# An encoder layer with a mixture of experts: late conditioning chunks put ahead in three queues, a first chunk in halves, and the last expert block added on chip

## The chip, the cores and the metric

The kernel runs on one core of a Trainium2 chip. The metric is the device time of one execution in microseconds; less is better.

## The reference, cut to what matters

1536 tokens (a sequence of 512 and one of 1024) of width 1024, all in float32. Each sequence has its own conditioning row c.

```
mod = silu(c) @ w_ada + b_ada                 # six rows of 1024: shift1, scale1, gate1, shift2, scale2, gate2
h   = x * (1 + scale1) + shift1
z   = h @ w_in                                # 1536 columns: u | v | p
a   = gelu(u) * (w_spatial @ layernorm(gelu(v)) + b_spatial)    # chunks of 128 positions, 4 heads
b   = (windowed mean(p) - p) @ w_pool * pool_scale              # windows 2, 4, 8, 16
x   = layernorm(alpha * x + gate1 * ([a | b] @ w_out))
h   = x * (1 + scale2) + shift2
# each token goes to 2 of 32 experts (top group, top 2 inside it), rows grouped by expert in blocks of 128
y_e = (silu(h @ gate_e) * (h @ up_e)) @ down_e                  # gate, up: 1024 -> 512, down: 512 -> 1024
y   = sum over the token's two experts of weight * y_e
out = layernorm(alpha * x + gate2 * y)
```

## The kernel before

The five engines each run a program written out by hand, and meet only at semaphores; each engine takes its instructions in the order in which they stand. SyncE issues nearly all loads, GpSimd the indirect ones. A float32 product is made of three: each operand is split into a high half (rounded on ScalarE, the functions named high_) and a low half (subtracted on VectorE, the functions named low_), and TensorE adds high*high, high*low and low*high.

**Start.** Tiles of 128 tokens are taken in pairs, pair 0 first. For pair 0 the work goes by k, the eight slices of 128 input features: for each k a chunk of w_ada (load_ada0, in two DMAs; high_ada0; low_ada0; ada0_mm) gives shift1 and scale1 of these features, mod_columns turns them into columns, mods(k) adds the bias and modulates the slice of x, k_high and k_low split it, and the products with row k of w_in (load_win, high_win, low_win, three slots) follow. In front of k = 0 stand on TensorE some filler products (warm), the transposes of x tiles 0 and 1, the transpose of the bias columns, ada0_mm(0) and mod_columns(0). ScalarE copies the four banks of transposed x out of PSUM in between. VectorE's order from k = 0 on is mods(0), low_win(0), k_low(0), low_ada0(1), low_win(1), low_ada0(2), then for each k mods(k), low_win(k + 1), k_low(k), low_ada0(k + 2).

**Pairs 1 to 5.** TensorE makes u, p and v of the pair, and at four points of it, called u1, u3, p1 and p3, a late chunk: 256 further columns of w_ada for the other four rows of mod. There are twelve, n = 0 to 11: n = 3 at u3 of pair 1, n = 5 at p3 of pair 1, n = 7 at u3 of pair 2, n = 9 at p3 of pair 2. A late chunk is loaded (load_ada(n), which waits for late chunk n - 3 to be used), rounded (high_for), subtracted (low_late) and multiplied (late_mm, 16 products of 256 columns). ScalarE, VectorE and SyncE have the three steps each at a fixed place among their other work: VectorE's low_late(1, "u3") stands behind pool_p(0), the windowed sums of pair 0; high_for(i, "p3") stands behind high_h(2i + 2) on ScalarE and low_late(i, "p3") behind low_h(2i + 2) on VectorE, the split of the next pair's first tile; load_ada(9) stands behind load_x(7). After late_mm of u3, TensorE runs spatial(i - 1) and w_pool_mm(i - 1), and the latter waits for pool_p(i - 1).

**Norm, routing, experts.** The first layer norm goes tile by tile, with routing between. The rows h2 go to HBM, and a table gives for each block of 128 rows which rows it takes and where its result goes. The loop over blocks: gather(i) on GpSimd, transposes, gate_up(i) on TensorE, silu and gate, the transposes of the activations, down(i). take_y(i) on ScalarE copies the block's result to y_sb, and scatter(i) on GpSimd writes its rows to y_rows in HBM, one row for each token and choice. In the loop, TensorE runs gate_up(i), the transposes of block i + 1, down(i - 1), the transposes of block i's activations.

**End.** After the last block's down products ScalarE copies the result out, GpSimd scatters it, and SyncE loads y0 and y1 (the rows of both choices) for each of the twelve tiles in four slots once all scatters have landed. The twelve x1 tiles (fin) and four broadcast rows are loaded earlier, on the last blocks' progress. Meanwhile TensorE runs 36 filler products and ScalarE makes 24 diagonal matrices of the token weights (diag, in place of scaling rows). For each tile TensorE adds diag0 @ y0 + diag1 @ y1 in two halves of 512 columns, four plain float32 products, and VectorE gates it, adds alpha * x1, and makes the second layer norm; ScalarE squares and stores.

## Time and profile before

| | us |
|---|---|
| median of 3 runs | 1309.48 (1307.46 to 1310.91) |
| the profiled execution, its own time | 1311.05 |
| its span | 1309.3 |
| TensorE busy in it | 1242.0 (95%) |
| VectorE busy | 949.5 (73%) |
| ScalarE busy | 643.5 (49%) |
| GpSimd busy | 201.8 (15%) |
| granted TensorE clock, mean | 0.973 of full |

Start times count from the span's start. A wait in brackets behind an instruction is the idle time of its engine just before it, with what ended it. The pair stage runs from about 83 to 315, the norm and routing to about 530, the expert loop to 1225, the end from there. Records of products overlap: a product's record is longer than the distance to the next.

### The profile page before, as it was taken

To read this page: it belongs to the slowest core of one execution; us is meant where nothing else is said; L and a number is where in the kernel's file an instruction comes from. 1 tells how busy PE (TensorE), PEld (TensorE's weight loads), DVE (VectorE), ACT (ScalarE), POOL (GpSimd) and SP (SyncE) were. 2 spreads that over 40 slices of the span, in tenths; PEclk is the share of its full clock that TensorE was granted. 3 is DMA by queue.
4 is the path that set the end of the run, shared out by engine and by line. 5 is a ranking of instruction groups with operands and counts; after the bars stand their busy time and mean duration, and the time that the engine had idled before them with its cause. 6 is when DMAs were issued, how large, how long until landed. Compare 5 with 4: busy or idle time off the path is not lost.

```text
span 1309.3 us, 23427 instructions
## 1 busy us (share of the span) xinstructions
PE 1242.0 (95%) x6534; PEld 1026.6 (78%) x6535; DVE 949.5 (73%) x1180; ACT 643.5 (49%) x667; POOL 201.8 (15%) x242
## 2 busy tenths in 40 slices
PE   7998989999999999899999999999999999999890
PEld 6887979998888874778888888888888888888640
DVE  4765655556999987874788656664899988887297
ACT  5552221123222223655677545744777887776421
POOL 0011101000010011121112111111121221121122
PEclk8998989999999998899999999999999999999896
DMA  9942231015423456965999757765999999998983
GB/s 312 273 129 82 81 97 53 19 57 179 146 113 115 175 219 260 362 242 218 353 390 406 284 219 295 273 256 215 366 390 402 397 406 395 393 402 294 353 306 128
DMA packets 121646, 329.09 MB, mean 251 GB/s; under 512 B 12040, under 2 KB 43904, under 8 KB 121604
## 3 DMA queue, kind: packets, MB, share of 16 engines
q1 hardware_dynamic: 107412, 288.08, 59.1%
q0 software_dynamic: 12320, 34.15, 7.3%
q10 hardware_dynamic: 1872, 6.29, 1.2%
q8 instruction: 27, 0.44, 0.1%
q14 instruction: 15, 0.12, 0.0%
HBM read 296.97 MB, written 39.42 MB: 257 GB/s over the span
## 4 chain that ended last, share of the span: by engine, by line
PE 66%; DVE 16%; issue 11%; DMA 3%; POOL 2%; ACT 2%; DVEq 0%; ACTq 0%; SPq 0%; POOLq 0%
PE bank L1603 17%; PE bank L1605 17%; PE bank L1604 17%; PE bank L1903 2%; PE bank L1616 2%; PE bank L1618 2%; PE bank L1617 2%; POOL rstd L729 1%; PE bank L1927 1%; DVE h L1340 1%; DVE fin L1562 1%; DVE fin L1577 1%; ACT w_mid L945 1%; DVE gated L1558 1%; DMA sh2b<-mod_rows 1%
## 5 line engine op out<-in xcount | busy, mean ns | idle before, releaser
L1476 DVE TENSOR_TENSOR gu_l<-gu_raw,gu_h (+1 forms) x128 | 287.3, 2285 | 44.0 <-ACT gu_h L971 41.9
L1603 PE MATMUL bank<-gu_h,xT_h 128*128 (+1 forms) x624 | 247.3, 396 | 2.8 <-issue 1.4
L971 ACT ACTIVATE gu_h<-gu_raw (+1 forms) x128 | 238.9, 1928 | 14.1 <-issue 12.8
L1605 PE MATMUL bank<-gu_h,xT_l 128*128 (+1 forms) x624 | 243.8, 391 | 0.0
L1604 PE MATMUL bank<-gu_l,xT_h 128*128 (+1 forms) x624 | 243.4, 390 | 0.0
L1480 DVE TENSOR_TENSOR dn_l<-dn_raw,dn_h (+1 forms) x64 | 143.6, 2285 | 5.9 <-ACT dn_h L975 5.9
L1603 PEld LDWEIGHTS bank<-gu_h,xT_h 128*128 128x128 f32 x624 | 117.6, 188 | 26.7 <-issue 3.1
L1605 PEld LDWEIGHTS bank<-gu_h,xT_l 128*128 128x128 f32 x624 | 117.5, 188 | 25.1
L1604 PEld LDWEIGHTS bank<-gu_l,xT_h 128*128 128x128 f32 x624 | 117.7, 189 | 23.3
L1603 PE MATMUL bank<-dn_h,aT_h 128*128 (+1 forms) x312 | 125.5, 402 | 2.5 <-DVE aT_l L1490 2.5
L1605 PE MATMUL bank<-dn_h,aT_l 128*128 (+1 forms) x312 | 122.3, 392 | 0.0
L1604 PE MATMUL bank<-dn_l,aT_h 128*128 (+1 forms) x312 | 122.2, 392 | 0.0
L975 ACT ACTIVATE dn_h<-dn_raw (+1 forms) x64 | 119.0, 1914 | 0.1
L1616 PE MATMUL bank<-hT_h,win_h 128*128 128x256 f32 x384 | 110.0, 286 | 6.0 <-DVE hT_l L1135 5.5
L981 ACT ACTIVATE act_s<-bank 128x512 f32<-128x512 f32 x39 | 23.3, 597 | 181.2 <-PE bank L1605 181.2
L1618 PE MATMUL bank<-hT_h,win_l 128*128 128x256 f32 x384 | 107.8, 281 | 0.0
L1617 PE MATMUL bank<-hT_l,win_h 128*128 128x256 f32 x384 | 107.7, 281 | 0.0
L758 POOL DMA_INDIRECT y_rows<-y_sb,s_idx x39 | 72.6, 1862 | 192.1 <-ACT y_sb L1001 192.1
L1486 DVE TENSOR_TENSOR act_a<-bank,act_s 128x512 f32<-128x512 f32 x39 | 26.9, 691 | 79.5 <-ACT act_s L981 79.5
L1616 PEld LDWEIGHTS bank<-hT_h,win_h 128*128 128x128 f32 x384 | 72.9, 190 | 8.3 <-DVE hT_l L1135 6.5
L1603 PE MATMUL bank<-wout_h,z_h 128*128 128x512 f32 x192 | 77.4, 403 | 0.0
L1605 PE MATMUL bank<-wout_h,z_l 128*128 128x512 f32 x192 | 75.9, 395 | 0.0
(278 smaller groups left out, 2156.5 us busy)
## 6 DMA issues: line engine op xcount, KB each, us to landing
gu_raw<-in_w_gate_up SPq DMA_DIRECT2D x128, 1024.0 KB, 7.8
dn_raw<-in_w_down SPq DMA_DIRECT2D x64, 1024.0 KB, 7.5
y<-y_rows SPq DMA_DIRECT2D x24, 512.0 KB, 5.5
ada_raw<-in_w_ada SPq DMA_DIRECT2D x20, 512.0 KB, 7.1
ada_raw<-in_w_ada SPq DMA_DIRECT2D x10, 1024.0 KB, 5.6
win_raw<-in_w_in SPq DMA_DIRECT2D x8, 768.0 KB, 8.8
h_rows<-h SPq DMA_DIRECT2D x12, 512.0 KB, 2.6
fin<-x_rows SPq DMA_DIRECT2D x12, 512.0 KB, 9.3
```

The lines of the kernel that those rows point to most:

```text
L758: nc.gpsimd.indirect_dma_start(out=y_d, out_offset=bass.IndirectOffsetOnAxis(ap=s_idx[:, 0:1], axis=0), in_=y_sb[:], in_offset=None, bound ...
L971: nc.scalar.activation(gu_slot(gu_h, e, c), gu_slot(gu_raw, e, c), ACT.Copy).then_inc(S["gu_split_h"], 1)
L975: nc.scalar.activation(dn_slot(dn_h, e, c), dn_slot(dn_raw, e, c), ACT.Copy).then_inc(S["dn_split_h"], 1)
L1476: nv.tensor_tensor(gu_slot(gu_l, e, c), gu_slot(gu_raw, e, c), gu_slot(gu_h, e, c).bitcast(F32), ALU.subtract).then_inc(S["gu_split_l"], 1)
L1480: nv.tensor_tensor(dn_slot(dn_l, e, c), dn_slot(dn_raw, e, c), dn_slot(dn_h, e, c).bitcast(F32), ALU.subtract).then_inc(S["dn_split_l"], 1)
L1486: nv.tensor_tensor(act_a[:], ps[1][:], act_s[:], ALU.mult).then_inc(S["act_ready"], 1)
L1603: mm(out, lh, rh, start=start, stop=False)
L1604: mm(out, lh, rl, start=False, stop=False)
L1605: return mm(out, ll, rh, start=False, stop=stop)
L1616: mm(out, win_h[:, k, c], hT_h[s][:, k, :], start=start, stop=False)
L1617: mm(out, win_h[:, k, c], hT_l[s][:, k, :], start=False, stop=False)
L1618: return mm(out, win_l[:, k, c], hT_h[s][:, k, :], start=False, stop=stop)
```

## The change

1. **Late chunks.** load_ada(9) goes ahead of load_x(7) on SyncE; high_for(i, "p3") ahead of high_h(2i + 2) on ScalarE (for the last pair there is no such chunk); low_late(1, "u3") ahead of pool_p(0), and low_late(i, "p3") ahead of low_h(2i + 2), on VectorE.
2. **First chunk by halves.** The two DMAs of chunk 0 get a semaphore each, and rounding and subtraction are done in two halves. TensorE runs ada0_mm(0) ahead of the x transposes. Slice 0 of x is modulated straight out of PSUM; ScalarE copies the banks without it, two before k_high(0) and two after it. Row 0 of w_in is split in two parts (u columns first), and k_low(0) stands ahead of the second part.
3. **Last block.** It isn't scattered. clear_last, on GpSimd between gather(3) and scatter(0), writes zeros to the rows of y_rows that it would have written; this counts as one scatter, so every scatter and take_y waits for one more, and SyncE's loads of y0 and y1 wait for the clear and for the scatters of all blocks but the last. VectorE makes a 0/1 matrix onehot (which token each row of the last block belongs to) from an index row that GpSimd makes, and finds each row's weight through row_sel, its transpose on TensorE between the two halves of the last down product, and one small product. ScalarE scales the result into last_h, VectorE makes last_l, and TensorE adds onehot @ last_h and onehot @ last_l to every tile, four more products of 512 columns. The 36 filler products go; the diagonal matrices are made before the last block's result is taken.

```diff
+    " x_loaded xT_made x0_ready x0_used ada_first ada_h_made ada_l_made ada_made mod_hl_made mod_cols mod_made"
...
                 c, n = 2 * D + (k - KD) * ADA_N + m * P, P
-            sp.dma_start(ada0_raw[slot][:, :, m * P:(m + 1) * P], w_ada[:, :, c:c + n]).then_inc(ada_loaded[slot], 16)
+            sp.dma_start(ada0_raw[slot][:, :, m * P:(m + 1) * P], w_ada[:, :, c:c + n]).then_inc(S["ada_first"] if k + m == 0 else ada_loaded[slot], 16)
...
     load_ada(8)
+    load_ada(9)
     load_x(7)
-    load_ada(9)
     load_ada(10)
...
+    def clear_last():
+
+        pool.wait_ge(S["tab_ready"], 3)
+        st.done(pool.memset(y_sb[:], 0.0))
+        st.done(nc.gpsimd.tensor_copy(s_idx[:], table_s[:, bass.ds(column(last_block), 1)]))
+        st.sync()
+        nc.gpsimd.indirect_dma_start(out=y_d, out_offset=bass.IndirectOffsetOnAxis(ap=s_idx[:, 0:1], axis=0),
+                                     in_=y_sb[:], in_offset=None, bounds_check=PAIRS - 1,
+                                     oob_is_err=False).then_inc(S["y_scattered"], 16)
+
     def scatter(i):
-        if not (isinstance(i, int) and i == 0):
-            pool.wait_ge(S["y_scattered"], 16 * i)
+        pool.wait_ge(S["y_scattered"], 16 * i + 16)
         nc.gpsimd.tensor_copy(s_idx[:], table_s[:, bass.ds(column(i), 1)]).then_inc(S["y_idx"], 1)
...
     gather(3)
-    pool.wait_ge(S["tab_ready"], 2)
+    clear_last()
     scatter(0)
...
         scatter(i - 1)
-    scatter(last_block)
+    nc.gpsimd.iota(iota_t[:], pattern=[[1, T]], base=0, channel_multiplier=0,
     pool.wait_ge(S["gathered"], 16 * (n_blocks + 2))
...
+    def high_first(m):
+        act.wait_ge((S["ada_first"], ada_loaded[0])[m], 16)
+        part = slice(m * P, (m + 1) * P)
+        nc.scalar.activation(ada0_h[0][:, :, part], ada0_raw[0][:, :, part], ACT.Copy).then_inc(S["ada_h_made"], 1)
+
     def high_ada0(k):
         slot = k % ADA0_SLOTS
-        act.wait_ge(ada_loaded[slot], 32 * (k // ADA0_SLOTS + 1))
+        act.wait_ge(ada_loaded[slot], 32 * (k // ADA0_SLOTS + 1) - (16 if slot == 0 else 0))
         if k >= 2:
...
-    high_ada0(0)
-    act.wait_ge(S["xT_made"], 2)
-    for b in range(4):
-        nc.scalar.activation(h_raw[0][:, 4 * (b % 2):4 * (b % 2) + 4, b // 2 * P:(b // 2 + 1) * P],
-                             ps[b][:].rearrange("p (k m) -> p k m", k=4), ACT.Copy).then_inc(S["x0_ready"], 1)
-    act.wait_ge(S["colsT_made"], 1)
-    nc.scalar.activation(cols[:], ps[7][:, 0:NCOL], ACT.Copy).then_inc(S["cols_ready"], 1)
+    for m in range(2):
+        high_first(m)
+
+    def copy_x0(b):
+        first = 1 if b % 2 == 0 else 0
+        nc.scalar.activation(h_raw[0][:, 4 * (b % 2) + first:4 * (b % 2) + 4, b // 2 * P:(b // 2 + 1) * P],
+                             ps[b][:, first * P:].rearrange("p (k m) -> p k m", k=4 - first), ACT.Copy).then_inc(S["x0_ready"], 1)
...
         act.wait_ge(win_loaded[k % WIN_SLOTS], 16 * (k // WIN_SLOTS + 1))
-        nc.scalar.activation(win_h[:, k, :], win_raw[k % WIN_SLOTS][:], ACT.Copy).then_inc(S["win_h_made"], 1)
+        for part in ((slice(0, AW), slice(AW, 3 * AW)) if k == 0 else (slice(0, 3 * AW),)):
+            nc.scalar.activation(win_h[:, k, part], win_raw[k % WIN_SLOTS][:, part], ACT.Copy).then_inc(S["win_h_made"], 1)
...
     mod_hl_out(0)
+    act.wait_ge(S["colsT_made"], 1)
+    nc.scalar.activation(cols[:], ps[7][:, 0:NCOL], ACT.Copy).then_inc(S["cols_ready"], 1)
     high_win(0)
+    act.wait_ge(S["xT_made"], 2)
+    copy_x0(1)
+    copy_x0(3)
     k_high(0)
+    act.wait_ge(S["x0_used"], 3)
+    copy_x0(0)
+    copy_x0(2)
     high_ada0(1)
...
         row_out(i, "p1")
+        high_for(i, "p3")
         if i < NP - 1:
...
             high_wout(0)
-        high_for(i, "p3")
         copy_p(i, 1)
...
         act.wait_ge(S["dn_used"], 2 * i + 2)
-        if not (isinstance(i, int) and i == 0):
-            act.wait_ge(S["y_scattered"], 16 * i)
+        act.wait_ge(S["y_scattered"], 16 * i + 16)
         for b in range(2):
...
         expert_block(i)
-    take_y(last_block)
     for t in range(NT):
...
     last.then_inc(S["w_act"], 1)
+    act.wait_ge(S["list_dve"], 8)
+    act.wait_ge(S["dn_used"], 2 * last_block + 2)
+    for b in range(2):
+        nc.scalar.activation(last_h[:, 512 * b:512 * (b + 1)], ps[5 + b][:], ACT.Copy, scale=last_w[:, 0:1]).then_inc(S["w_act"], 1)
...
         slot = k % ADA0_SLOTS
-        dve.wait_ge(S["ada_h_made"], k + 1)
+        dve.wait_ge(S["ada_h_made"], k + 2)
         nv.tensor_tensor(ada0_l[slot][:], ada0_raw[slot][:], ada0_h[k % 2][:].bitcast(F32), ALU.subtract).then_inc(S["ada_l_made"], 1)
+    def low_first(m):
+        dve.wait_ge(S["ada_h_made"], m + 1)
+        part = slice(m * P, (m + 1) * P)
+        nv.tensor_tensor(ada0_l[0][:, :, part], ada0_raw[0][:, :, part], ada0_h[0][:, :, part].bitcast(F32), ALU.subtract).then_inc(S["ada_l_made"], 1)
+
     def low_win(k):
-        dve.wait_ge(S["win_h_made"], k + 1)
-        nv.tensor_tensor(win_l[:, k, :], win_raw[k % WIN_SLOTS][:], win_h[:, k, :].bitcast(F32), ALU.subtract).then_inc(S["win_l_made"], 1)
+        dve.wait_ge(S["win_h_made"], k + 2)
+        part = slice(AW if k == 0 else 0, 3 * AW)
+        nv.tensor_tensor(win_l[:, k, part], win_raw[k % WIN_SLOTS][:, part], win_h[:, k, part].bitcast(F32), ALU.subtract).then_inc(S["win_l_made"], 1)
+
+    def low_win_u():
+        dve.wait_ge(S["win_h_made"], 1)
+        nv.tensor_tensor(win_l[:, 0, 0:AW], win_raw[0][:, 0:AW], win_h[:, 0, 0:AW].bitcast(F32), ALU.subtract).then_inc(S["x0_used"], 1)
...
         high_gain(k)
-        modulate_k(0, k, h_raw[0][:, k, :]).then_inc(S["k_mod"], 1)
+        if k == 0:
+            dve.wait_ge(S["xT_made"], 2)
+            for a in range(2):
+                nv.tensor_scalar(h_raw[0][:, 0, a * P:(a + 1) * P], ps[2 * a][:, 0:P], gain1[:, 0, 0:1], mod[:, 0, 0:1],
+                                 ALU.mult, ALU.add).then_inc(S["x0_used"], 1)
+            dve.wait_ge(S["x0_used"], 3)
+            dve.sem_inc(S["k_mod"], 1)
+        else:
+            if k == 1:
+                dve.wait_ge(S["x0_ready"], 4)
+            modulate_k(0, k, h_raw[0][:, k, :]).then_inc(S["k_mod"], 1)
...
-    low_ada0(0)
+    for m in range(2):
+        low_first(m)
     dve.wait_ge(S["cols_ready"], 1)
-    dve.wait_ge(S["x0_ready"], 4)
+    low_win_u()
     mods(0)
+    k_low(0)
     low_win(0)
-    k_low(0)
     low_ada0(1)
...
     norm_v(1)
+    low_late(1, "u3")
     pool_p(0)
-    low_late(1, "u3")
     for i in range(1, NP):
...
             modulate(2 * i + 2)
+            low_late(i, "p3")
             low_h(2 * i + 2)
-            low_late(i, "p3")
             modulate(2 * i + 3)
...
         step(nv.reciprocal(wts[:, 0, :], den[:]))
-        step(nv.tensor_tensor(wts[:, 1, :], wts[:, 0, :], ex[:], ALU.mult))
+        nv.tensor_tensor(wts[:, 1, :], wts[:, 0, :], ex[:], ALU.mult).then_inc(S["tab_ready"], 1)
...
+    last_block = dve.value_load(block_n[0:1, 1:2], min_val=NE - 1, max_val=MAXBLK - 1)
+    last_col = dve.value_load(block_c[0:1, bass.ds(last_block, 1)], min_val=0, max_val=COLS - 1)
+    last_s = table_s[:, bass.ds(last_col, 1)]
+    dve.wait_ge(S["xT_l_made"], n_blocks + 1)
+    st.done(nv.tensor_scalar(last_i[:, 0:1], last_s, P - 1, None, ALU.bitwise_and))
+    st.done(nv.tensor_scalar(last_i[:, 1:2], last_s, 7, None, ALU.logical_shift_right))
+    step(nv.tensor_copy(last_f[:, 2:3], last_s))
+    st.done(nv.tensor_copy(last_f[:, 0:2], last_i[:]))
+    step(nv.tensor_scalar(last_f[:, 3:4], last_f[:, 2:3], float(T), -float(T), ALU.is_ge, ALU.mult))
+    dve.wait_ge(S["rt_consts"], 11)
+    nv.tensor_scalar(row_sel[:], iota_t[:, 0:P], last_f[:, 0:1], None, ALU.is_equal).then_inc(S["list_dve"], 1)
+    st.done(nv.tensor_scalar(col_sel[:], iota_t[:, 0:2 * NT], last_f[:, 1:2], None, ALU.is_equal))
+    step(nv.tensor_tensor(last_f[:, 2:3], last_f[:, 2:3], last_f[:, 3:4], ALU.add))
+    nv.tensor_scalar(onehot[:].rearrange("p t m -> p (t m)"), iota_t[:], last_f[:, 2:3], None, ALU.is_equal).then_inc(S["list_dve"], 1)
+    dve.wait_ge(S["list_pe"], 4)
+    nv.tensor_copy(row_selT[:], ps[7][:, 0:P]).then_inc(S["list_dve"], 1)
+    dve.wait_ge(S["list_pe"], 5)
+    nv.scalar_tensor_tensor(col_w[:], ps[7][:, 0:2 * NT], 1.0, col_sel[:], ALU.mult, ALU.mult, accum_out=last_w[:, 0:1]).then_inc(S["list_dve"], 1)
+    for b in range(2):
+        c = slice(512 * b, 512 * (b + 1))
+        dve.wait_ge(S["w_act"], 3 + b)
+        nv.scalar_tensor_tensor(last_l[:, c], ps[5 + b][:], last_w[:, 0:1], last_h[:, c].bitcast(F32), ALU.mult, ALU.subtract).then_inc(S["list_dve"], 1)
...
             pe.wait_ge(S["h_ready"], 2)
-        pe.wait_ge(S["ada_l_made"], k + 1)
+        pe.wait_ge(S["ada_l_made"], k + 2)
         for kk in range(KD):
...
     warm(5, 17)
+    pe.wait_ge(S["c_low"], 2)
+    ada0_mm(0)
     pe.wait_ge(S["x_loaded"], 32)
     transposes(0, 0, xs)
-    transposes(1, 2, xs_b)
     pe.wait_ge(S["rows_loaded"], 48)
     nc.tensor.transpose(ps[7][:, 0:NCOL], col_rows[:], ident[0:NCOL, 0:NCOL]).then_inc(S["colsT_made"], 1)
-    pe.wait_ge(S["c_low"], 2)
-    ada0_mm(0)
+    transposes(1, 2, xs_b)
     mod_columns(0)
...
         pe.wait_ge(S["k_low"], k + 1)
-        pe.wait_ge(S["win_l_made"], k + 1)
+        if k > 0:
+            pe.wait_ge(S["win_l_made"], k + 1)
         first, end = k == 0, k == KD - 1
+        if first:
+            pe.wait_ge(S["x0_ready"], 3)
         for j in range(4):
...
             next_pair(KD - 1, 7)
+        if first:
+            pe.wait_ge(S["win_l_made"], 1)
         for half in range(2):
...
                 last.then_inc(S["v_made"], 1)
+        if first:
+            pe.wait_ge(S["x0_ready"], 4)
         for j in range(4):
...
-    def down(i, e):
+    def down(i, e, halves=range(2)):
         pe.wait_ge(S["aT_l_made"], i + 1)
         pe.wait_ge(S["y_ready"], i + 1)
-        for c in range(2):
+        for c in halves:
             pe.wait_ge(S["dn_split_l"], 2 * e + c + 1)
...
         a_transposes_e(i)
-    down(last_block, NE - 1)
+    down(last_block, NE - 1, (0,))
+    pe.wait_ge(S["list_dve"], 5)
+    nc.tensor.transpose(ps[7][:, 0:P], row_sel[:], ident[:]).then_inc(S["list_pe"], 1)
+    down(last_block, NE - 1, (1,))
+    pe.wait_ge(S["list_dve"], 7)
+    mm(ps[7][:, 0:2 * NT], row_selT[:], wts[:].rearrange("p c t -> p (c t)"), start=True, stop=True).then_inc(S["list_pe"], 1)
     pe.wait_ge(S["dn_split_l"], 2 * NE)
-    warm(7, 36)
     pe.wait_ge(S["w_act"], 2)
...
             mm(ps[bank + b][:], diag[:, 0, t, :], y0[slot][:, n], start=True, stop=False)
-            mm(ps[bank + b][:], diag[:, 1, t, :], y1[slot][:, n], start=False, stop=True).then_inc(S["y_summed"], 1)
+            mm(ps[bank + b][:], diag[:, 1, t, :], y1[slot][:, n], start=False, stop=False)
+            if t == 0:
+                pe.wait_ge(S["list_dve"], 9 + b)
+            mm(ps[bank + b][:], onehot[:, t, :], last_h[:, n], start=False, stop=False)
+            mm(ps[bank + b][:], onehot[:, t, :], last_l[:, n], start=False, stop=True).then_inc(S["y_summed"], 1)
```

## Rows read from the trace of the kernel before

**Rows 1.** Waits of TensorE, 90 to 330 us: us in total, times, longest.

```profile
PE bank L1657 <- DVE ada_l L1172: 10.4, 3, 5.3
```

**Rows 2.** Timeline of TensorE: start us, us, instruction, idle before in brackets.

```profile
102.17 0.28 PE L1657 MATMUL bank<-ada_h,c_hl 128*4 128x256 f32 x1 [2.67 <-DVE ada_l L1172]
...
125.58 0.28 PE L1657 MATMUL bank<-ada_h,c_hl 128*4 128x256 f32 x1 [2.45 <-DVE ada_l L1172]
...
179.80 0.37 PE L1657 MATMUL bank<-ada_h,c_hl 128*4 128x256 f32 x1 [5.31 <-DVE ada_l L1172]
```

**Rows 3.** Chain that ended last, pair stage: start us, us, what.

```profile
105.21 2.35 PE bank L1666 x16
...
114.83 0.11 PE bank L1657
...
116.66 0.89 PE bank L1610 x8
...
128.15 1.71 PE bank L1610 x8
...
156.12 1.78 PE bank L1666 x16
...
183.37 1.62 PE bank L1610 x8
```

**Rows 4.** Timeline of the other queues around the three waits.

```profile
92.92 1.90 ACT L856 ACTIVATE ada_h<-ada_raw 128x2048 fp32r<-128x2048 f32 x1
...
93.72 1.32 DVE L1221 TENSOR_TENSOR abuf<-pbuf 128x1116 f32<-128x1116 f32 x1
...
99.74 2.28 DVE L1172 TENSOR_TENSOR ada_l<-ada_raw,ada_h 128x2048 fp32r<-128x2048 f32 x1
...
121.21 1.90 ACT L856 ACTIVATE ada_h<-ada_raw 128x2048 fp32r<-128x2048 f32 x1
...
169.30 1.12 SPq L485 DMA_DIRECT2D ada_raw<-in_w_ada  x2
...
175.42 1.91 ACT L856 ACTIVATE ada_h<-ada_raw 128x2048 fp32r<-128x2048 f32 x1 [2.76 <-DMA ada_raw<-in_w_ada]
```

**Rows 5.** Start: TensorE, ScalarE, and the load of win_raw issued at 18.5.

```profile
18.76 0.58 PE L1616 MATMUL bank<-hT_h,win_h 128*128 128x256 f32 x1 [3.01 <-DVE hT_l L1135]
...
27.89 1.47 ACT L823 ACTIVATE win_h<-win_raw 128x1536 fp32r<-128x1536 f32 x1
...
L463 SPq DMA_DIRECT2D win_raw<-in_w_in x1: 432/432/432, 18.5 to 18.5; - x1
...
DMA to landing us min/median/max: 8.3/8.3/8.3
```

**Rows 6.** Timeline where clear_last will stand, in the first blocks.

```profile
559.73 1.08 ACT L1001 ACTIVATE y_sb<-bank 128x512 f32<-128x512 f32 x2
...
561.72 2.91 POOL L758 DMA_INDIRECT y_rows<-y_sb,s_idx  x1 [3.17 <-ACT y_sb L1001]
...
572.49 0.47 PE L1603 MATMUL bank<-dn_h,aT_h 128*128 x1
```

**Rows 7.** Timeline of the end.

```profile
1225.35 0.18 POOL L754 COPY s_idx<-table_s 128x1 int32 x1 [7.45 <-DMA y_rows<-y_sb,s_idx]
...
1230.37 0.33 SPq L662 DMA_DIRECT2D y<-y_rows  x1
...
1235.50 1.48 PE L1974 MATMUL bank<-y,diag 128*128 128x512 f32 x2 [2.42 <-DMA y<-y_rows]
...
1247.65 1.28 DVE L1558 TENSOR_TENSOR gated<-bank,g2b 128x512 f32<-128x512 f32 x2
...
1252.75 1.28 DVE L1558 TENSOR_TENSOR gated<-bank,g2b 128x512 f32<-128x512 f32 x2
```

**Rows 8.** Stretches of the end: us, busy PE, PEld, DVE, ACT, POOL, clock, DMA, GB/s.

```profile
1236.00:1238.00 2.00, 2.00 (x4) 0.93 (x3) 0.00 (x0) 0.00 (x0) 0.00 (x0) 0.52 1.03 416
...
1250.00:1260.00 10.00, 10.00 (x24) 4.37 (x23) 9.86 (x17) 2.48 (x4) 3.04 (x2) 1.00 0.93 289
```

More of the change, by code:

```diff
@@ L385, in encoder @@
             " edge_iota spl_ones"
-            " x_loaded xT_made x0_ready ada_h_made ada_l_made ada_made mod_hl_made mod_cols mod_made"
+            " x_loaded xT_made x0_ready x0_used ada_first ada_h_made ada_l_made ada_made mod_hl_made mod_cols mod_made"
             " k_mod k_high k_low win_h_made win_l_made h_ready hT_h_made hT_l_made"
@@ L775, in _ @@
                 scatter(i - 1)
-            scatter(last_block)
+            nc.gpsimd.iota(iota_t[:], pattern=[[1, T]], base=0, channel_multiplier=0,
+                           allow_small_or_imprecise_dtypes=True).then_inc(S["rt_consts"], 1)
             pool.wait_ge(S["gathered"], 16 * (n_blocks + 2))
```

15 lines of the change are left out of this document (added).

## The prediction

> **What bounds the kernel now.** I read the page first: its slices say which engine is full in each stretch (TensorE nearly everywhere; VectorE alone in the layer norms and at the end). Then the waits of TensorE by stretch, then the instructions in order of time around each wait, on all queues, to see what came last. In the pair stage, 90 to 330 us, TensorE waits for one thing only, the low half of a late conditioning chunk, three times, 10.4 us in all [rows 1]. The three are u3 of pair 1, p3 of pair 1 and p3 of pair 2 [rows 2]. Everything else there is TensorE's own work, so what these waits lose is lost to the end: the norms, the routing and the expert loop that follow start from what TensorE has finished. After the loop, the end is first a chain (last block, scatter, reload) and then VectorE's work per tile.
>
> **Part 1, the late chunks.** At u3 of pair 1, ScalarE has the high half at 92.92 + 1.90 = 94.82; VectorE is free at 93.72 but takes pool_p(0) first, 93.72 to 99.74, and subtracts only then (2.28) [rows 4]; TensorE waits 2.67 [rows 2]. With the subtraction first it runs 94.9 to 97.1, and TensorE asks for it at 102.17 - 2.67 = 99.5: no wait. pool_p(0) then ends its part that TensorE needs at about 97.1 + 5.9 = 103.0. What is late next is w_pool_mm(0): TensorE comes to it after the sixteen chunk products (1.83) and the spatial products (1.78), at 99.5 + 3.6 = 103.1. That is just enough; I cost it at nothing, with 0.3 as the bound. At p3 of pair 1 ScalarE rounds the chunk at 121.21, behind high_h of tile 4 [rows 4]; moved ahead it follows the p1 row copy, some 8 us earlier. VectorE then subtracts right behind modulate(4). In the shifted time of part 1, transposes end at 113.3, modulate(4) at 115.9, the subtraction at 118.2, and TensorE asks at 118.8: no wait, slack 0.6. The high_h/low_h pair behind it comes 1 to 2 us later and is needed only by the next pair. At p3 of pair 2 it is the load: SyncE issues it at 169.30, behind load_x(7) which waits for tile 6's transposes; it lands for ScalarE at 175.42 [rows 4]. Its own wait (u3 of pair 2 done) is met near 156, so ahead of load_x(7) it lands about 13 us earlier; the one instruction passed, load_x(7), waits for a later event than the load now ahead of it, so it isn't delayed. Rounding and subtraction are then bound by modulate(6), as at pair 1, and end some 0.6 before TensorE asks. All three waits go: 2.67 + 2.45 + 5.31 = 10.4.
>
> They take TensorE's clock with them. Sixteen chunk products take 116.66 - 114.83 = 1.83 at full clock, eight transposes 0.89, the sixteen spatial products 1.78 [rows 2, 3]. The chunk products begin at the end of each wait, and the group of the chain's row follows: u3, 102.17 to 107.56 = 5.39 for work of 3.61, 1.78 lost; p3 of pair 1, 125.58 to 129.86 = 4.28 for 2.72, 1.56 lost; p3 of pair 2, 179.80 to 184.99 = 5.19 for 2.72, 2.47 lost. Together 5.8. Part 1 gives 10.4 + 5.8 = 16.2. Bounds: 10.4 (if the clock falls all the same) less 0.3, and 16.2.
>
> **Part 2, the start.** TensorE begins the first products at 18.76 after a wait of 3.01 [rows 5]. With the first chunk in halves and ada0_mm(0) ahead of the x transposes, the subtraction ends near 9.4 instead of 11.5 and the conditioning products near 11.3; mod_columns(0) comes when the x transposes are through, near 14.0; one add, one gain and two modulates of half size make 14.9, k_high 15.7, k_low 16.1. So k = 0 can start 2.6 us earlier. But the next step is held by a load: win_raw of k = 2 is issued at 18.5 and lands 8.3 later, at 26.8, whatever the engines do, since SyncE's queue ahead of it is unchanged; VectorE has low_win(2) in front of k_low(1), and ScalarE rounds that row only at 27.89 [rows 5]. Only 27.89 - 26.8 = 1.1 of the shift gets through to k = 1. Later k follow from it by TensorE's own work. I take 1.1; bounds 0 and 2.6.
>
> **Part 3, the cleared rows.** clear_last stands between gather(3) and scatter(0): a memset, an index copy and an indirect write of 128 rows; take_y(0) waits for its landing. Now take_y(0) starts at 559.73 and TensorE needs block 1's activations at 572.49 [rows 6]. GpSimd is done with gather(3) about 558.4; memset and copy put the issue near 560.4. In the fullest stretch of the trace a block scatter kept GpSimd waiting 7.45 us behind its issue of about 1.1 [rows 7]; I take these 8.6 as the upper bound of the landing, 569.0, and about half as the lower, 564.7. take_y (1.1), high_aT (0.6) and low_aT (0.7) follow: 567.1 to 571.4, before 572.49. Hidden, behind gate_up(2); if that cover is gone, each us costs one. ScalarE's next work, silu(2), is at 571.9.
>
> **Part 4, the end.** Now: the last down product ends at 1225.0, its scatter is issued, y loads begin at 1230.37, the first sum starts at 1235.50 [rows 7]: 5.13 from issue to sum. After: the loads need the clear and the scatters up to block n-2. That last one is still slow, for GpSimd, waiting for it, moves on at 1225.35 (7.45 idle) [rows 7]; the twelve x1 tiles and four broadcasts fill the queue then. So y loads begin near 1225.3, not when the last gate_up ends, and the first sum at 1225.3 + 5.1 = 1230.4. The block's own data is earlier: row_sel (index steps from 1217.6, iota after the last scatter issue) is ready near 1220.6, its transpose stands between the down halves at 1221.8; after the last product come one small product, col_w 0.4, two scaled copies 1.1, two subtractions, last_l complete by 1228. Diag copies (7.1 on ScalarE) move under the down products. All hidden by the load, with over 2 us to spare.
>
> Then the sums. Before, 24 records in 10 us [rows 8] are 8 a tile, 3.43 us; four new products of 512 columns at twice the 0.115 of a 256-column one add 0.9: 4.34 per tile. VectorE takes 1252.75 - 1247.65 = 5.10 per tile [rows 7], so it stays the bound once it runs without gaps. The opening is slower, though: before, the first sum came 2.42 us after the filler products [rows 7] and the clock was low all the same (0.52) [rows 8]; now the fillers are gone and the idle time is 5 us, as at p3 of pair 2, so I take it low for 5 us from the first sum. Tile 0's halves end at 1234.8 and 1237.3, tile 1's at 1239.5 and 1241.6, tile 2's at 1243.8 and 1246.0. VectorE, with its 1.23 + 1.28 of full-row work between, starts tile 2 at 1245.1 and its second half at 1246.0, 2.2 before the present 1247.65 (by the second halves). From there all is as before. I take 2.2; bounds 0 (loads two us later) and 5.8 (full clock, loads 0.7 earlier).
>
> **Sum.** 16.2 + 1.1 + 2.2 = 19.5. The profiled execution took 1311.05 (span 1309.3), which becomes 1291.5; it stands 1.57 above the median of the runs, 1309.48, so the forecast is 1290.0.
>
> **Rivals.**
> 1. Part of the wait comes back (pooled at pair 0, or modulate in front of the subtraction, slack 0.1 and 0.6). If one short site keeps its wait and clock loss, 2.45 + 1.56 = 4.0 to 4.4 return; two sites, 8.5: 1294 to 1298.5. For it: the slacks are small. Against: a returning wait would be tenths, not the whole.
> 2. The end gives all it can, 5.8, and the start 2.6: 1285.
> 3. The clear is late. GpSimd's scatter issue took 2.91 at 561.72 [rows 6] while VectorE was subtracting, and about 1 elsewhere. If the issue waits until VectorE pauses near 565.9 and lands 5.2 later, TensorE waits 1 and loses clock 1.5: 1292.5. The Trainium skill (SBUF — State Buffer, section "SBUF: two separate sides", its note on VectorE blocking DMAs) says that descriptors of a GpSimd DMA can't be written while VectorE runs an operation holding the shared port; that rule would give this rival, and the row's 2.91 leans its way without showing the cause.
> 4. The other side: TensorE becomes the bound of the final sums. It decides from 5.10 us per tile, that is, from 0.42 for each new product. If these run like the old ones (0.86) a tile is 6.9, 11 x 1.8 = 19 more: 1309, no change. If TensorE, no longer dense, stays at the low clock, a tile is 8.7, 11 x 3.6 = 39 more: 1329. Against: 85% busy from 1235 on.
> 5. The shift is not passed on, because some transfer between 315 and 530 us is late anyway: 1306 to 1309. Against: these loads are all issued on TensorE's progress.
>
> **Chances.** Forecast 0.60 (own range 1286.5 to 1294), rival 1 0.15, rival 2 0.09, rival 3 0.06, rival 4 0.06 (of it slower 0.04), rival 5 0.04. The range reaches over rivals 1 to 3: 1284 to 1298.5. Within 0.3% is within 3.9 us of 1309.5, about what the runs can tell. Faster 0.91, same 0.05, slower 0.04.
>
> **What the changed profile would show.** No TensorE wait on ada_l in the pair stage, and granted clock 1.0 from 100 to 190 us; w_pool_mm(0) without a wait. First product near 16.2, but k = 1 near 30.4. take_y(0) near 565 to 570 with no TensorE gap at the second down. First y load near 1206 in the new time (19.5 us less than 1225.3), first sum 5 us behind it, VectorE at 5.1 per tile. Wrong if TensorE's records per tile in the end spread over more than 5.1, or if w_pool_mm(0) or the p3 products wait over 1 us.

## The result

The changed kernel took 1295.16 us (median of 4 runs, 1293.76 to 1296.26), the kernel before 1310.2 beside it (4 runs, 1307.46 to 1311.05). The ratio is 0.9886, 95% interval 0.9872 to 0.9900: 15.0 us faster. Timed once more, later, it was 1293.91 (4 runs) beside 1311.07 (9 runs), ratio 0.9861 (0.9843 to 0.9880): 17.2 faster. The profiled executions, 1311.05 before and 1293.76 after, stand 17.3 apart. I had forecast 1290.0, 19.5 below the first median, with a range of 1284 to 1298.5.

**The pair stage.** The windows of the changed kernel over the stretches in which TensorE waited before (columns: busy time of TensorE, its weight loads, VectorE, ScalarE, GpSimd; granted clock; DMA share; GB/s):

```profile
95.00:112.00 17.00, 17.00 (x141) 15.71 (x140) 13.39 (x26) 4.29 (x7) 2.35 (x3) 1.00 0.30 94
122.00:136.00 14.00, 14.00 (x79) 12.06 (x79) 11.75 (x28) 4.07 (x4) 0.56 (x1) 1.00 0.32 110
170.00:179.00 9.00, 9.00 (x41) 7.23 (x40) 7.54 (x21) 3.46 (x3) 0.00 (x0) 1.00 0.07 28
179.00:192.00 13.00, 13.00 (x113) 12.51 (x112) 5.18 (x10) 1.57 (x3) 2.67 (x4) 1.00 0.27 81
```

TensorE is busy for the whole of each stretch and the granted clock is 1.00: the three waits of [rows 1] are gone, and the longest left anywhere between 83 and 320 us is one of 0.4, for another tile. I measure the stage from VectorE's first subtraction in it (85.21 before, 84.52 after) to SyncE's load of ln_g (314.89 and 297.84): 229.68 before, 213.32 after, 16.4 less.

**The start.** In order of time, TensorE's instructions that waited; they answer to [rows 5]:

```profile
16.88 0.38 PE L1701 MATMUL bank<-hT_h,win_h 128*128 128x256 f32 x1 [2.20 <-DVE hT_l L1197]
24.16 0.60 PE L1725 MATMUL bank<-pair_sum,mod_hl 4*128 4x2 f32 x4 [0.79 <-ACT mod_hl L850]
26.32 0.37 PE L1718 MATMUL bank<-ada_h,c_hl 128*4 128x256 f32 x1 [1.56 <-DVE ada_l L1158]
30.31 0.39 PE L1701 MATMUL bank<-hT_h,win_h 128*128 128x256 f32 x1 [0.77 <-DVE hT_l L1197]
```

The first products come 1.88 earlier (16.88 for 18.76), those of k = 1 1.24 earlier (30.31 for 31.55), the pair stage 0.69. The load holds k = 1 as forecast: ScalarE begins to round row k = 2 of w_in at 26.64, as soon as it lands, where it came to it at 27.89 before [rows 5].

**The clear.** GpSimd's and ScalarE's rows around it, which answer to [rows 6]:

```profile
541.39 0.97 POOL L770 MEMSET y_sb<- 128x1024 f32 x1
542.29 2.30 POOL L771 COPY s_idx<-table_s 128x1 int32 x1
545.44 2.21 POOL L773 DMA_INDIRECT y_rows<-y_sb,s_idx  x1 [0.85 <-POOL s_idx L771]
```
```profile
550.53 1.09 ACT L1040 ACTIVATE y_sb<-bank 128x512 f32<-128x512 f32 x2 [6.98 <-DMA y_rows<-y_sb,s_idx]
551.50 0.60 ACT L1025 ACTIVATE aT_h<-bank 128x512 fp32r<-128x512 f32 x1
```

take_y(0) waits 6.98 for the clear's landing, and TensorE shows no wait for it. The clear is slow for its size: the copy of 128 indices takes 2.30 and the issue 2.21, where the same two take 0.18 and 1.00 for the next block; VectorE was subtracting all through. That agrees in direction with the Trainium skill (SBUF — State Buffer, section "SBUF: two separate sides"), by which VectorE can hold a port that GpSimd and its descriptors need; no run here took VectorE's work away, so the cause isn't shown. The time is hidden anyway.

**The end.** The changed kernel in order of time: SyncE's last broadcast, GpSimd's last scatter, the y loads, TensorE's first sum, VectorE's first rows; they answer to [rows 7]:

```profile
1195.12 1.36 SPq L671 DMA_DIRECT2D ln_bb<-in_ln_b  x1
...
1207.39 0.33 SPq L678 DMA_DIRECT2D y<-y_rows  x1
```
```profile
1199.65 1.11 POOL L783 DMA_INDIRECT y_rows<-y_sb,s_idx  x1 [4.47 <-ACT y_sb L1040]
```
```profile
1215.02 2.04 PE L2070 MATMUL bank<-y,diag 128*128 128x512 f32 x2 [8.42 <-DMA y<-y_rows]
```
```profile
1207.67 1.41 DVE L1634 SCALAR_TENSOR_TENSOR last_l<-bank,last_w,last_h 128x512 fp32r<-128x512 f32 x2 [0.84 <-ACT last_h L1100]
1219.73 0.69 DVE L1643 TENSOR_TENSOR gated<-bank,g2b 128x512 f32<-128x512 f32 x1 [10.65 <-PE bank L2075]
...
1235.44 1.28 DVE L1643 TENSOR_TENSOR gated<-bank,g2b 128x512 f32<-128x512 f32 x2
```

last_l is complete at 1209.1, but the first sum comes at 1215.02. It waits for y loads issued at 1207.39, 7.63 earlier; before, this flight took 5.13 [rows 7]. The loads wait for the last scatter, issued at 1199.65, so 7.7 before them. What stands in the queue then is seen in the DMA issues from 1180 to 1212 (columns: count, size of one, median us from issue to landing) and in the windows (the last two columns are DMA share and GB/s, the one ahead of them the clock):

```profile
fin<-x_rows SPq DMA_DIRECT2D x12, 512.0 KB, 9.5
y<-y_rows SPq DMA_DIRECT2D x8, 512.0 KB, 8.7
...
ln_bb<-in_ln_b SPq DMA_DIRECT2D x1, 512.0 KB, 17.2
```
```profile
1206.00:1209.00 3.00, 0.60 (x5) 0.42 (x3) 1.52 (x4) 1.55 (x3) 0.00 (x0) 1.00 1.03 419
1212.00:1215.00 3.00, 0.00 (x0) 0.01 (x1) 0.00 (x0) 0.00 (x0) 0.00 (x0) 0.50 1.03 414
1215.00:1218.00 3.00, 2.98 (x5) 1.44 (x5) 0.00 (x0) 0.00 (x0) 0.00 (x0) 0.50 1.03 410
1218.00:1222.00 4.00, 4.00 (x9) 1.99 (x9) 0.69 (x1) 0.00 (x0) 0.00 (x0) 0.72 0.67 267
```

The last broadcast lands 17.2 after its issue at 1195.12, at 1212.3, so the y loads of 1207.39 stand behind it in SyncE's queue. The two other traces with this order of loads and the matrix in which the flight can be read have 7.42 (e3_last) and 7.70 (e11_after); the ten traces with the last block scattered, or with the new order of loads told below, have 5.03 to 5.25. And TensorE, idle for 8.4 us, begins the sums at half clock (0.50). From the start of the last down block to VectorE's last group of f_scale rows (1299.95 and 1282.65) the end takes 82.28 us before and 82.08 after: the last block added on chip gained 0.2.

### The profile page after: what moved, and what is told of

Its sections match the earlier page's. It is cut to its first block, busy times and chain, and to the rows that moved or that the text cites. A ratio compares the mean times of both kernels' runs of the same rounds, so it can differ in the third digit from the quotient of the medians.

```text
span 1292.0 us, 23415 instructions
## 1 busy us (share of the span) xinstructions
PE 1238.0 (96%) x6513; PEld 1021.3 (79%) x6514; DVE 954.9 (74%) x1197; ACT 643.8 (50%) x669; POOL 205.6 (16%) x244
## 4 chain that ended last, share of the span: by engine, by line
PE 73%; DVE 15%; issue 4%; DMA 3%; ACT 2%; POOL 2%; SPq 2%; ACTq 0%; DVEq 0%; POOLq 0%
PE bank L1688 18%; PE bank L1690 18%; PE bank L1689 18%; PE bank L1701 3%; PE bank L1703 3%; PE bank L1702 3%; PE bank L1995 3%; POOL rstd L745 1%; PE bank L2019 1%; DVE h L1403 1%; ACT w_mid L985 1%; DVE fin L1647 1%; DVE fin L1662 1%; DVE gated L1643 1%; DMA sh2b<-mod_rows 1%
## 5 line engine op out<-in xcount | busy, mean ns | idle before, releaser
L783 POOL DMA_INDIRECT y_rows<-y_sb,s_idx x38 | 70.0, 1843 | 186.0 <-ACT y_sb L1040 186.0
```

Of the source, the lines that this page charges most:

```text
L783: nc.gpsimd.indirect_dma_start(out=y_d, out_offset=bass.IndirectOffsetOnAxis(ap=s_idx[:, 0:1], axis=0), in_=y_sb[:], in_offset=None, bound ...
```

## The experiments

All times are beside runs of the kernel before on the same chip: it took 1310.35 (21 runs) beside e1 to e4, 1309.25 (9) beside e5 to e8, 1311.07 (9) beside e9 to e11, and 1310.5 (9) beside e12.

### One part at a time

e1_late holds the moves of load_ada(9), high_for(i, "p3"), low_late(1, "u3") and low_late(i, "p3") and nothing else:

```diff
 load_ada(8)
+load_ada(9)
 load_x(7)
-load_ada(9)
...
+high_for(i, "p3")
 if i < NP - 1:
     high_h(2 * i + 2)
 else:
     high_wout(0)
-high_for(i, "p3")
...
+low_late(1, "u3")
 pool_p(0)
-low_late(1, "u3")
...
+low_late(i, "p3")
 low_h(2 * i + 2)
-low_late(i, "p3")
```

e2_start holds the diff's lines on ada_first, x0_used, copy_x0, low_win_u and the order of TensorE's opening; e3_last those on clear_last, last_h, last_l, onehot and row_sel.

> The kernel before with part 1 alone: load_ada(9) ahead of load_x(7), high_for(i, p3) ahead of high_h, low_late(1, u3) ahead of pool_p(0), low_late(i, p3) ahead of low_h. My theory (the three waits of TensorE on the low halves are gone, 10.4 us, and the low clock behind them with them, 5.8 us): -16.2 us beside the kernel before, no wait over 0.5 us of TensorE between 83 and 320 us, no stretch at the low clock there. In the trace of the whole change this stage gave 16.38 us. Rival (the parts need each other, so that the shift is not passed on or the waits come back at the next site): -10 or less.

Measured: 1295.65 (4 runs), ratio 0.9889 (0.9874 to 0.9904), -14.7 us. From the first subtraction of the pair stage to the load of ln_g 213.34 us, as in the whole change. This part alone makes the changed kernel's time as first measured (-15.0); against the later -17.2 it is 2.5 short.

> The kernel before with part 2 alone: the first chunk by halves, ada0_mm(0) ahead of the transposes, the first modulation read from PSUM. My theory: the start gives what the trace of the whole change shows, 0.67 us at the first product of the pair stage, with 1.24 us gained at the second chunk and half of it lost again by the landing of w_in's rows; so -0.5 to -1.2 us. Rival (a shift at the start is swallowed by the waits on late chunks of the pair stage, which hang on loads that no step here has moved): 0.

Measured: 1311.13 (11 runs), ratio 1.0008 (0.9999 to 1.0017): +0.8, no gain. The rival's 0 is at the edge of the interval, my -0.5 to -1.2 outside. The trace of this run shows the rival at work. The pair stage starts at 84.30, 0.9 before the kernel before, and TensorE asks for the low half at p3 of pair 2 at 173.75 instead of 174.49. But the load, issued at 168.57 instead of 169.30, lands for ScalarE only at 176.55 instead of 175.42, and TensorE waits 7.18 instead of 5.31:

```profile
180.93 0.37 PE L1692 MATMUL bank<-ada_h,c_hl 128*4 128x256 f32 x1 [7.18 <-DVE ada_l L1207]
```

That is one trace; why the load took longer isn't shown. What else becomes of the 1.24 us at k = 1 is told with part 2 below.

> The kernel before with part 3 alone: clear_last, the last block added by the 0/1 matrix, no scatter of it. In the whole change the stretch from the last down block to the third tile's products gave only 0.2 us of the 2.2 that I forecast, since the first y loads took 7.6 us from issue to the first sum and not 5.1. My theory: -0.2 us, between -2.2 and +0.5. Rival (the clear of y_sb and the extra scatter ahead of the first block cost time that the whole change hides under part 1's shift): +1 to +3.

Measured: 1309.07 (11 runs), ratio 0.9997 (0.9987 to 1.0007): -1.3 by the medians, and no difference by the interval, in which my -0.2 lies and the rival's +1 to +3 does not.

### The order of SyncE's last loads

```diff
-            for t in range(NT):
-                sp.dma_start(fin[t][:], x1_d[...]).then_inc(x1_loaded[t // 4], 16)
+            def load_fin(lo, hi):
+                for t in range(lo, hi):
+                    sp.dma_start(fin[t][:], x1_d[...]).then_inc(x1_loaded[t // 4], 16)
+
+            load_fin(0, 4)
             sp.wait_ge(S["gu_used"], 4 * n_blocks)
...
             (four broadcasts, wait for the scatters, then per tile t: y0, y1)
+                if t == F_SLOTS - 1:
+                    load_fin(4, 8)
+                if t == F_SLOTS:
+                    load_fin(8, NT)
```

> The changed kernel with SP's loads of the end in another order: four tiles of x1, the four broadcasts, the y loads of tiles 0 to 3, and only then the other eight tiles of x1 (4 MB). Theory A (the gain of part 3 was lost in the DMA queues: the scatter of the last block but one, issued at 1199.65, landed 7.7 us later and the first y loads another 7.6, both behind 8.3 MB of x1 and broadcasts): the scatter lands in 2 to 4 us, y loads issue at 1202 to 1204, and the first sum comes with last_l's end at about 1209.5 and no longer at 1215.0; 4 to 5.5 us faster than the changed kernel, so 19 to 21 us faster than before. Theory B (the scatter and the y loads are slow by themselves, an indirect scatter of 512 KB takes near 8 us anyway): within 1.5 us of the changed kernel. Theory C (the eight late tiles of x1 now keep the fused residual of tile 4 or 8 waiting): the first sum is early, and the end is not.

Measured: 1287.33 (5 runs, 1286.05 to 1290.44), ratio 0.9826 (0.9813 to 0.9840), -23.0 us, where the changed kernel has -15.0 and -17.2: 6 to 8 us ahead of it. That is Theory A, and more than its 5.5. Of e4_order, SyncE's first y load, TensorE's first sum with VectorE's first row, and the windows:

```profile
1206.01 0.33 SPq L681 DMA_DIRECT2D y<-y_rows  x1
```
```profile
1211.15 1.10 PE L2077 MATMUL bank<-y,diag 128*128 128x512 f32 x2 [0.48 <-DMA y<-y_rows]
1213.66 0.69 DVE L1650 TENSOR_TENSOR gated<-bank,g2b 128x512 f32<-128x512 f32 x1 [0.52 <-PE bank L2082]
```
```profile
1203.00:1206.00 3.00, 2.85 (x7) 2.27 (x8) 2.33 (x10) 3.00 (x12) 1.79 (x2) 0.50 0.46 183
1206.00:1209.00 3.00, 3.00 (x15) 2.37 (x14) 0.76 (x2) 2.87 (x10) 0.00 (x0) 0.94 0.64 197
1212.00:1215.00 3.00, 3.00 (x10) 1.51 (x8) 1.84 (x3) 0.28 (x1) 0.00 (x0) 1.00 1.01 403
```

The scatter issued at 1202.24 frees the y loads at 1206.01, 3.8 us later and not 7.7, and their flight is 5.14 and not 7.63 (in the three other kernels with this order and the matrix, 3.8 to 4.7 and 5.1). Counted from the last down block's start (1203.15 here, 1200.57 in the changed kernel) the first sum comes at 8.0 instead of 14.45, 6.45 earlier. The other 2.6 of the 9.0 us by which this trace's end is shorter are the clock: TensorE idled 0.5 us, not 8.4, and the sums begin at 1.00 (e9_warm_end below prices this by itself). The Trainium skill (DMA: Bandwidth & Descriptors, section "Queues, rings and completion order") says that each DMA engine takes an issuer's descriptors in the order of its ring; the changed kernel's trace agrees, with the last broadcast landing at 1212.3 and the first sum, which waits for the later y loads, at 1215.02.

e7_late_order has this edit on e1_late, e8_no_start has it on the kernel before with e1_late's and e3_last's lines.

> Part 1 alone with SyncE's loads of the end in the order of e4_order, but the last block still scattered and read back. It says what the 0/1 matrix is worth once the queues are clear. In e4_order the first sum began 8.0 us behind the last down product's beginning (1203.15 to 1211.15). Here the scatter of the last block leads: last down products 7 us, copy to y_sb 1.1, scatter issue 1 and landing near 3, y loads 4 to 5: first sum 16 to 17 us behind the last down block's beginning, where e1_late had 18.2. Theory A (the matrix is worth most of what e4_order gained): 1 to 3 us faster than e1_late, so -16 to -18 beside before, and e4_order stays 5 to 6 us ahead. Theory B (the order of the loads is the gain, with the matrix or without): 6 to 8 us faster than e1_late.

Measured: 1294.0 (4 runs, 1293.18 to 1299.14), ratio 0.9893 (0.9866 to 0.9920), -15.3 us, 0.6 more than e1_late's -14.7; in the traces its end is 1.3 us shorter (81.41 for 82.69). Theory A, and below its low end; the interval, -10.5 to -17.5 us, is wide, so the size rests on the trace. Neither step is worth much by itself: the matrix in the old order 0.2 us of the end, the order without the matrix 1.3. Both together give 9.2 in e4_order (82.28 less 73.07) and 6.8 to 8.5 in the three other traces that have them (e8_no_start 75.44, e12_spread 73.94, e10_order_warm 73.81). By the medians it is 7 to 8 (e8_no_start's -21.9 and e4_order's -23.0 beside e1_late's -14.7). Without the matrix the last block's scatter and its landing still lie in the chain, whatever the queue holds.

> Parts 1 and 3 with the new order of SyncE's loads, without part 2. Theory A (part 2 is worth nothing: in the four traces at hand the subtraction of the first chunk of the pair stage begins at 84.30 and 84.32 without it, at 84.28 and 84.52 with it): the same time as e4_order, 23 us beside before, within 1 us. Theory B (it is worth the 1.1 us that I forecast): 1 us slower than e4_order.

Measured: 1287.31 (4 runs, 1285.85 to 1289.38), ratio 0.9831 (0.9810 to 0.9851), -21.9 us beside e4_order's -23.0, with the same time in us. The intervals overlap; Theory A stands, but they don't exclude that part 2 is worth about one us. (The expectation gives 84.30 as a start without part 2. It is e2_start's, which has it; without it the two traces of that time had 84.32 and 84.42.) The end also differs between traces of this order: here the last down block starts at full clock, TensorE then waits 2.65 for the y loads, the first sums run at 0.67 and 0.76, and the end takes 75.44 us instead of 73.07.

### The sites of part 1

e5_no_load9 is e1_late without the first of its four moves, e6_u3_only the kernel before with the third alone.

> Part 1 alone, but with load_ada(9) left where it was, behind load_x(7). My theory (each of the three sites is worth its own wait and its own low clock, and they add up): of the 14.7 us of part 1, 5.31 + 2.47 = 7.8 us are gone again, so -7 us beside the kernel before; TensorE waits some 5.3 us for the low half of p3 of pair 2 and has a granted clock of about 0.5 for some 5 us behind it; the two other sites stay without a wait. Rival (with ScalarE's and VectorE's steps ahead, the late load costs less, since the rounding and the subtraction no longer stand behind it): -10 to -12 us and a wait of 2 to 3 us.

Measured: 1303.19 (5 runs), ratio 0.9949 (0.9932 to 0.9967), -6.1 us. TensorE's waits from 84 to 320 us, and its clock behind the wait:

```profile
PE bank L1657 <- DVE ada_l L1172: 5.8, 1, 5.8
```
```profile
166.00:169.00 3.00, 0.00 (x0) 0.00 (x0) 0.12 (x1) 2.06 (x2) 0.00 (x0) 0.76 1.00 313
169.00:172.00 3.00, 0.69 (x4) 0.46 (x5) 3.00 (x2) 1.28 (x2) 0.00 (x0) 0.50 0.01 4
172.00:175.00 3.00, 3.00 (x19) 2.00 (x18) 0.31 (x1) 0.24 (x1) 0.00 (x0) 0.60 0.00 0
```

The stage takes 220.66 us, 7.3 more than e1_late's 213.34, for 7.8 forecast. The site is worth its wait and the low clock behind it.

> The kernel before with low_late(1, u3) ahead of pool_p(0) and nothing else. My theory: the wait of 2.67 us at u3 of pair 1 is gone with 1.78 us of low clock behind it, the two p3 waits (2.45 and 5.31) stay as they are: -4.4 us. Rival (the next wait grows by what this one loses, since ScalarE and VectorE don't come earlier with TensorE): -1 to -2 us, and the wait at p3 of pair 1 is 4 to 5 us.

Measured: 1305.34 (5 runs), ratio 0.9961 (0.9946 to 0.9976), -3.9 us, near the 4.4 expected. In the trace the stage takes 223.42, 6.3 us less than before, and later stages lose some of it again (from the load of ln_g to the first of w_down 205.67 for 203.52, the end 83.13 for 82.28). The waits at p3 stay (2.46 and 5.65), but the clock differs: TensorE's instruction behind the first of them, and the windows,

```profile
121.02 0.28 PE L1657 MATMUL bank<-ada_h,c_hl 128*4 128x256 f32 x1 [2.46 <-DVE ada_l L1172]
```
```profile
119.00:122.00 3.00, 0.98 (x9) 0.77 (x10) 1.87 (x1) 0.19 (x1) 0.00 (x0) 1.00 0.01 2
122.00:125.00 3.00, 3.00 (x23) 2.58 (x22) 1.08 (x4) 0.37 (x1) 0.79 (x1) 1.00 0.13 12
...
173.00:176.00 3.00, 2.04 (x10) 1.23 (x11) 0.82 (x1) 0.00 (x0) 0.00 (x0) 0.50 0.00 0
```

show 1.00 behind a wait of 2.46, where the same wait, 2.45, was followed by half clock before (1.56 us lost, [rows 2]); 2.67 + 1.78 + 1.56 = 6.0, near the 6.3. Behind the wait of 5.65 the clock was low again. In the four traces that keep this wait, 2.40 to 2.46 us long, the clock fell in three. A short wait may or may not cost the clock; only its chance can be forecast, not its 1.6 us.

### Filler products

```diff
 e9_warm_end, on the changed kernel, ahead of the final sums:
+warm(4, 72)
 e10_order_warm, on e4_order:
 g2_part(1, 2)
+warm(1, 20)
 route(NT - 1)
...
+warm(7, 18)
 down(last_block, NE - 1, (0,))
 e12_spread, on e4_order: warm(1, 11) and warm(7, 10) there, and in SyncE's loop
-if t == F_SLOTS:
-    load_fin(8, NT)
+if F_SLOTS <= t < 2 * F_SLOTS:
+    load_fin(t + 4, t + 5)
```

> The changed kernel itself, timed beside the two others of this call and beside the kernel before: the base for both. It also says how much the runs of one kernel differ by the low clock in the routing stage (476 to 500 us), which was 0.93 there in the profile of after and 0.79 in that of e4_order, with 2.9 us between them at the end of that stage. Expected 1294 to 1296, -15 beside before.

Measured: 1293.91 (4 runs: 1292.89, 1293.81, 1294.01, and 1296.83, the one with a profile). Where that run lost its 3 us is told below.

> The changed kernel with 72 filler products (128 columns, some 8 us) behind the last small product, where TensorE is idle from 1206.6 to 1215.0. My theory (the clock was 0.50 from 1212 to 1218 and 0.72 up to 1222, since TensorE idled 8.4 us, and this costs the opening of the final sums some 2 us until VectorE, at 5.11 us a tile, is the bound): the clock stays at 1.00 in the opening, the first sum comes when the y loads land as before, and the first two halves of gated follow 1.1 and 3.3 us behind it, where they were 4.7 and 7.2: 2 to 3 us faster than the changed kernel. Rival (VectorE starts earlier, and then waits for y tiles or x1 tiles in the full queue): under 1 us.

Measured: 1299.58 (5 runs), ratio 0.9910 (0.9893 to 0.9927), -11.5 us, so 5.7 slower than the changed kernel beside it. A filler is two records on the engine, and 72 of them take not 8 us but 16:

```profile
1206.06 16.32 PE L1684 MATMUL bank<-ident 128*128 128x128 f32 x144
1222.22 1.02 PE L2071 MATMUL bank<-y,diag 128*128 128x512 f32 x2
```
```profile
1224.67 0.69 DVE L1643 TENSOR_TENSOR gated<-bank,g2b 128x512 f32<-128x512 f32 x1 [15.98 <-PE bank L2076]
```

I had taken the time of a transpose for them. The kernel as a whole is a miss, but its trace answers the question: with the clock at 1.00 the end takes 65.0 us from the first sum (1222.22) to VectorE's last row (1287.22), the changed kernel 67.6 (1215.02 to 1282.65). TensorE shows no wait for a y tile in either opening behind the first sum. The low clock in the opening costs 2.6 us, within the 2 to 3 expected.

> e4_order with 20 filler products ahead of the last tile's router products (TensorE idles 2.83 us there) and 18 ahead of the last down block (2.54 us idle). Theory A (what spreads the runs of one kernel is whether these two idle gaps lower the clock: 16 router products took 3.60 us in the profile of e4_order and 1.95 in that of after, and the last down products ran at 0.50 from 1203 to 1206 in e4_order and at 1.00 in after): the clock is at 1.00 in both places in every run, and the median falls by 2 to 4 us to 1283 to 1285, with a spread under 1.5 us. Theory B (the clock falls there for what TensorE did earlier, or the spread comes from elsewhere): the same 1287 with a spread of 4 us.

Measured: 1287.6 (5 runs, 1286.36 to 1290.43), ratio 0.9820 (0.9802 to 0.9838), -23.5 us. The mean granted clock is 0.987 or 0.988 in all five runs, where e4_order's had been 0.982 to 0.985, and yet the time is the same with the same spread: Theory B by the numbers. The trace shows two new losses, fillers that outlast their gap and a wait for a y tile behind x1 tiles:

```profile
476.62 4.73 PE L1691 MATMUL bank<-ident 128*128 128x128 f32 x40
481.19 1.87 PE L1918 MATMUL bank<-router_w,h2T 128*128 128x36 f32 x16
```
```profile
1232.94 1.73 PE L2079 MATMUL bank<-y,diag 128*128 128x512 f32 x2 [2.30 <-DMA y<-y_rows]
```

> e4_order once more, with the filler products sized to the gaps and the last four tiles of x1 loaded one behind each of the y tiles 4 to 7. In e10_order_warm one filler took 0.236 us, not the 0.12 that I had read off: the twenty in the routing stage lasted 4.7 us in a gap of 2.8 and held the router products up by 1.1, the eighteen ahead of the last down block ended level with their wait, and TensorE waited 2.3 us for a y tile behind the four x1 tiles. Now 11 fillers (2.6 us) and 10 (2.4 us). Theory A (these three are what ate e10_order_warm's gain): the router products take 1.95 us in each run, the last down block starts at full clock, no wait for a y tile over 0.5 us, and the median is 1284 to 1286. Theory B (fillers gain nothing, for where the clock stays full by them it would mostly have stayed so, or VectorE's rows bind all the same): 1286.5 to 1288.

Measured: 1288.44 (5 runs, 1285.52 to 1290.93), ratio 0.9825 (0.9807 to 0.9844), -22.1 us. In the trace the router products take 1.95, the last down products run at full clock, and no y tile is waited for once the sums run, as Theory A asked; but the first sum waits 2.82, and the time isn't Theory A's either: it is 0.4 above Theory B's range. (The profiled execution also began the pair stage at 86.37, 2.1 later than e4_order's, of which more below.) Of the last down block and the first sum:

```profile
1203.50 0.50 PE L1695 MATMUL bank<-dn_h,aT_h 128*128 128x512 f32 x1 [0.31 <-DVE aT_l L1560]
1212.36 1.10 PE L2079 MATMUL bank<-y,diag 128*128 128x512 f32 x2 [2.82 <-DMA y<-y_rows]
```

The last down products end earlier, and TensorE then waits 2.82 for the y loads, issued at 1207.24: the end is now bound by scatter and reload of the last block but one, not by TensorE, as in e8_no_start. e4_order, e8_no_start, e10_order_warm and e12_spread can't be told apart, at 1287.3 to 1288.4; e4_order is the smallest step from the changed kernel that beats both.

## Why the prediction held, and where it was off

The time fell into the range; the forecast was 5 us too low by the first medians. The mechanism of part 1 held and carries nearly all of the gain. Of the forecast, 2.0 us of part 4 and about 1 of part 2 weren't there. Step by step:

- **Part 1, 16.2 forecast, 16.4 in the trace, -14.7 in the medians of e1_late alone.** Right at each site: no wait, clock 1.00, w_pool_mm(0) without a wait although its cover was one tenth. What doesn't hold in general is the clock's share, 5.8: e6_u3_only shows that a wait of 2.5 us takes the clock with it in one trace and not in another. The profiled executions of e1_late (1295.54) and of before (1311.05) stand 15.5 apart, though the load of ln_g comes 17.2 earlier: 1.4 are lost between the last store of x1 and the first load of w_down (22.60 for 21.22), where e1_late's last 16 router products ran at half clock (3.60 us), and 0.4 in the end.
- **Part 2, 1.1 forecast, nothing measured.** The rule that a load holds k = 1 was right (first products 1.88 earlier, k = 1 1.24 in this trace). But the pair stage's first subtraction began at 84.32 to 84.95 us in six kernels without part 2 and at 85.21 in the kernel before, median of the seven 84.47; in five traces with part 2 at 84.01 to 84.52, median 84.30: 0.2 us. In two more with it, e11_after and e12_spread, it began at 87.17 and 86.37. In e11_after TensorE's wait at k = 1 was 2.49, and the windows, first of the changed kernel and then of e11_after, differ by the clock alone:

```profile
30.00:45.00 15.00, 14.33 (x104) 12.11 (x104) 10.77 (x15) 7.79 (x7) 0.00 (x0) 1.00 1.12 325
```
```profile
30.51 0.38 PE L1701 MATMUL bank<-hT_h,win_h 128*128 128x256 f32 x1 [2.49 <-DVE hT_l L1197]
...
30.00:45.00 15.00, 14.49 (x82) 12.65 (x83) 7.81 (x10) 7.37 (x6) 0.00 (x0) 0.77 1.09 327
```

  Products moved ahead of a load that doesn't move can leave a longer wait in front of the load: without part 2 the wait at k = 1 was 0.95 to 1.46 in seven traces, with it 1.92 to 2.49 in four of seven. From 30 to 45 us the clock was 0.77 in two of these four (behind 2.49 and 1.95) and 1.00 in two (1.97 and 1.92), and 0.99 or 1.00 in the ten others. Where it was low the pair stage began 2.1 and 2.9 us behind the median of the other five, more than the part could gain. I had reckoned with the load and not with the clock. Seven traces on each side make this likely and don't prove it.
- **The clear, hidden: right.** The clear landed for take_y(0) at 550.53, which is 567.1 in the old time (16.6 on), between my 564.7 and 569.0.
- **The end, 2.2 forecast, 0.2 measured: the mis-sized term is the y loads' flight, 5.1.** The loads were issued 6.8 us behind the last down block's start, 0.8 sooner than forecast, but took 7.63. I had seen that the x1 tiles and broadcasts fill the queue, and used it for the scatter alone, while the 5.13 of the flight came from a trace in which the queue had run empty before the y loads (DMA share 0.32 in the two us ahead of them, 1.03 in the changed kernel). The rest was as written: TensorE 4.38 per tile (forecast 4.34), VectorE 5.11 and so the bound, the opening at low clock. From the first sum to the fourth tile 20.42 us for 17.25 before, 3.2 more; the forecast had 2.9. (Two slips in the working, without weight: rows 8's 24 records in 10 us make 3.3 us for 8, and the 3.43 comes from 0.86 for each product; rival 4's 11 x 1.8 is 20 and not 19.)
- **Rivals.** 1, 3, 4 and 5 didn't come. Rival 2's 5.8 us at the end were there to be had, and need a step that the change didn't make: with the new order the end is 6.8 to 9.2 us shorter than before's. The sum by the traces: 16.4 + 0.7 + 0.2 = 17.3, the difference of the two profiled executions.

## What to carry to other kernels

When a chain is shortened so that a load starts sooner, ask what is still in that load's queue at the new time: its flight in the old trace holds for the old queue. A data path taken off the chain and a queue put in order can each be worth about one us or less alone and seven to nine together, so test them together before either is dropped. And when a cheap move ahead only brings an engine sooner to a wait that stays, it can cost the clock more than it gains.
